# Gate matrices as two fp32r products per token in place of one fp32 product

## What is computed

```
cand = (v1[..., :, None] + v2[..., None, :]).reshape(T, PEER_HEADS, PEER_TOPK * PEER_TOPK)
sc, pos = lax.top_k(cand, PEER_TOPK)
e1 = jnp.take_along_axis(i1, pos // PEER_TOPK, axis=-1)
e2 = jnp.take_along_axis(i2, pos % PEER_TOPK, axis=-1)
experts = (e1 * PEER_NKEYS + e2).reshape(T, PEER_HEADS * PEER_TOPK)
gates = jax.nn.softmax(sc, axis=-1).reshape(T, PEER_HEADS * PEER_TOPK)
...
u = peer_u[ec]
a = jax.nn.gelu(jnp.einsum("ckd,cd->ck", u, hc).astype(jnp.float32)) * gc
vv = peer_v[ec]
return jnp.einsum("ck,ckd->cd", a.astype(vv.dtype), vv)
```

## Time and profile before

| | us |
|---|---|
| runs (3): median | 3059.06 |
| lowest, highest | 3058.15, 3063.45 |
| profiled execution, its own time | 3053.1 |
| its span | 3051.2 |
| first pass: gelu of tick 0 to gelu of tick 127 | 1821.87 to 2489.52 |
| TensorE, VectorE, ScalarE busy over the span | 2839.0, 2259.4, 1481.5 |

### The profile page before, as it was taken

The page is one execution under the profiler, slowest core; times in us unless marked ns, Lnnn a source line. Parts: engine busy times, 40 slices in busy tenths (PEclk is TensorE's granted clock), DMA queues, the critical chain, the costliest instruction groups (busy, mean ns, idle before and its releaser), DMA issues.

```text
span 3051.2 us, 37281 instructions
## 1 busy us (share of the span) xinstructions
PE 2839.0 (93%) x13623; PEld 2361.2 (77%) x13623; DVE 2259.4 (74%) x3019; ACT 1481.5 (49%) x1990; POOL 595.8 (20%) x478
## 2 busy tenths in 40 slices
PE   5979888999999879998999898999899989999998
PEld 3657756888888758776777678989899988888887
DVE  6465547888888753887854229999998868888886
ACT  4443236888788633544542433563756633333332
POOL 0200111111111100000000010033233444444442
PEclk7999998999999989999999999999999999999999
DMA  7544636999999633332333334477779999999995
GB/s 298 170 161 155 207 128 247 369 369 365 360 359 355 235 128 121 107 115 80 102 133 131 121 105 161 175 265 282 280 264 332 354 377 367 360 370 362 360 366 190
DMA packets 203692, 746.29 MB, mean 245 GB/s; under 512 B 24817, under 2 KB 78193, under 8 KB 146417
## 3 DMA queue, kind: packets, MB, share of 16 engines
q1 hardware_dynamic: 123568, 492.93, 44.8%
q0 software_dynamic: 56912, 179.26, 16.7%
q10 hardware_dynamic: 23024, 71.67, 6.1%
HBM read 670.80 MB, written 98.11 MB: 252 GB/s over the span
## 4 chain that ended last, share of the span: by engine, by line
PE 51%; DVE 19%; issue 6%; DMA 5%; ACT 4%; ACTq 0%; DVEq 0%; POOL 0%; POOLq 0%
PE PS L542 44%; DVE wlo L1856 4%; DMA gbuf<-in_peer_u_dram,IDX 3%; DVE hf L2606 2%; DVE oh L2592 2%; ACT whi L1194 1%; DVE hf L2618 1%; PE PS L996 1%; PE PS L1008 1%; PE PS L847 1%; ACT HH L1826 1%; PE PS L1121 1%; DVE zo L2362 1%; DVE sS L2645 1%; PE PS L1092 1%
## 5 line engine op out<-in xcount | busy, mean ns | idle before, releaser
L1856 DVE TENSOR_TENSOR wlo<-raw,whi 128x2048 fp32r<-128x2048 f32 x392 | 894.3, 2289 | 367.5 <-ACT whi L1194 330.8
L1194 ACT ACTIVATE whi<-raw 128x2048 fp32r<-128x2048 f32 x392 | 750.8, 1916 | 370.7 <-PE PS L542 310.3
L542 PE MATMUL PS<-HH,whi 128*128 128x512 f32 (+1 forms) x2056 | 790.0, 384 | 37.2 <-DVE wlo L1856 14.4
L542 PE MATMUL PS<-HH,wlo 128*128 128x512 f32 (+1 forms) x2056 | 754.2, 367 | 0.0
L542 PE MATMUL PS<-HL,whi 128*128 128x512 f32 (+1 forms) x2056 | 752.9, 366 | 0.0
L542 PEld LDWEIGHTS PS<-HH,whi 128*128 128x128 f32 x2056 | 392.4, 191 | 98.4 <-issue 21.2
L542 PEld LDWEIGHTS PS<-HL,whi 128*128 128x128 f32 x2056 | 392.4, 191 | 46.1 <-issue 7.7
L542 PEld LDWEIGHTS PS<-HH,wlo 128*128 128x128 f32 x2056 | 391.4, 190 | 42.9
L542 PE MATMUL PS<-whi,HH 128*128 128x512 f32 (+1 forms) x896 | 351.8, 393 | 22.0 <-DVE HL L2648 16.6
L542 PE MATMUL PS<-whi,HL 128*128 128x512 f32 (+1 forms) x896 | 347.1, 387 | 0.0
L542 PE MATMUL PS<-wlo,HH 128*128 128x512 f32 (+1 forms) x896 | 347.0, 387 | 0.0
(11 more groups left out here) (415 smaller groups left out, 3908.9 us busy)
## 6 DMA issues: line engine op xcount, KB each, us to landing
raw<-in_moe_dram SPq DMA_DIRECT2D x192, 1024.0 KB, 7.3
raw<-in_u_units_dram SPq DMA_DIRECT2D x64, 1024.0 KB, 6.5
raw<-in_v_units_dram SPq DMA_DIRECT2D x64, 1024.0 KB, 8.8
raw<-in_w_in_dram SPq DMA_DIRECT2D x44, 1024.0 KB, 5.2
raw<-in_w_ada_dram SPq DMA_DIRECT2D x24, 1024.0 KB, 5.7
acts_dram<-sS ACTq DMA_DIRECT2D x64, 384.0 KB, 5.7
gates_dram<-XT ACTq DMA_DIRECT2D x24, 1024.0 KB, 8.2
sS<-acts_dram SPq DMA_DIRECT2D x42, 384.0 KB, 7.3
```

The lines of the kernel that those rows point to most:

```text
L542: ins = t.matmul(dst, a, b, start=(first and n == 0), stop=(last and n == 2))
L1194: a.inc(a.e.activation(m.whi[p % HRING][:, :, :], m.raw[RAW_SLOT[load_of(p)]][:, :, :], ACT.Copy), "hi", p)
L1856: v.inc(v.e.tensor_tensor(m.wlo[h][:, :, :], m.raw[RAW_SLOT[load_of(p)]][:, :, :], m.whi[h][:, :, :].bitcast(F32), ALU.subtract), "lo_v", p)
```

## The change

- The weighting of a gate's first one-hot is made twice: with the weight's high half, written in place, and with its low half, written to the free columns of `HH` and `HL`. All one-hots are fp32r. TensorE multiplies both with the second one-hot and adds them up: two fp32r products in place of one fp32.
- For each tile, ScalarE makes an fp32r copy of the transposed weights, and VectorE subtracts it to get the low half (`glow`).
- The planner counts 700 instead of 1100 ns of TensorE for a gate step.
- A buffer (`e12`) shares the place of another; `eT` grows by 128 columns.

```diff
@@ peer_schedule
-            tensor += 1100
+            tensor += 700
@@ Plan
-                self.eT = [sb(s2, "eT", [128, 384]), self.rstd]
-                self.oh = sb(s2, "oh", [128, 4, 2, 4, 128])
+                self.eT = [sb(s2, "eT", [128, 512]), self.rstd]
+                self.oh = sb(s2, "oh", [128, 4, 2, 4, 128], F32R)
...
+    def oh_low(self, n, j):
+
+        return (self.HH, self.HL)[n % 4 // 2][:, 4 * (n % 2) + j, 0:TD]
@@ pe_gate_step
+            pe.wait_ge("glow", i - 1)
...
-            ins = t.matmul(m.PS[:, 5 + n % 3, 128 * k:128 * k + 128], m.oh[:, n % 4, 0, k, :],
-                           m.oh[:, n % 4, 1, k, :], start=True, stop=True)
+            for low, w in enumerate((m.oh[:, n % 4, 0, k, :], m.oh_low(n, k))):
+                ins = t.matmul(m.PS[:, 5 + n % 3, 128 * k:128 * k + 128], w, m.oh[:, n % 4, 1, k, :],
+                               start=(low == 0), stop=(low == 1))
@@ act_gate_step
+            a.wait_ge("weighted", 32 * (k - 1) - 1)
         a.inc(s.activation(m.eT[k % 2][:, 0:384], m.PS[:, 4, 0:384], ACT.Copy), "eT", i)
+        a.inc(s.activation(m.eT[k % 2][:, 384:512].bitcast(F32R), m.PS[:, 4, 256:384], ACT.Copy), "ghigh", i)
...
-        a.wait_ge("eT", TD // 128 + k)
+        a.wait_ge("glow", TD // 128 + k)
         for j in range(4):
             t = 256 + 4 * q + j
-            a.inc(s.activation(m.oh[:, n % 4, 0, j, :], m.oh[:, n % 4, 0, j, :], ACT.Copy,
-                               scale=m.eT[k % 2][:, t:t + 1]), "weighted_part" if j < 3 else "weighted", n)
+            row = m.oh[:, n % 4, 0, j, :]
+            a.inc(s.activation(m.oh_low(n, j), row.bitcast(F32), ACT.Copy, scale=m.eT[k % 2][:, t + 128:t + 129]),
+                  "weighted_part", n)
+            a.inc(s.activation(row, row.bitcast(F32), ACT.Copy, scale=m.eT[k % 2][:, t:t + 1]),
+                  "weighted_part" if j < 3 else "weighted", n)
@@ dve_gate_step
+        if q == 0:
+            v.wait_ge("ghigh", TD // 128 + k)
+            v.inc(v.e.tensor_tensor(eT[:, 384:512], m.PS[:, 4, 256:384], eT[:, 384:512], ALU.subtract), "glow",
+                  TD // 128 + k)
```

More of the change, by code:

```diff
@@ L223 @@
     "peer_a": "xrow sq5 root5",
-    "choice": "top pick gsub gt index onehot",
+    "choice": "glow top pick gsub gt index onehot",
     "conv_a": "mean csq cdev zaff zact fstep",
@@ L508, in __init__ @@
                 self.gt = sb(s2, "gt", [128, NT, 8, 16])
-                self.e12 = sb(s2, "e12", [128, 8, 16])
+                self.e12 = self.wkk[:, 0, :].rearrange("p (h k) -> p h k", h=8)
                 self.e1 = sb(s2, "e1", [128, NT, 8, 16])
@@ L2566, in dve_choice_step @@
         if i * 128 < TD:
-            v.inc(e.scalar_tensor_tensor(out=m.e12[:, :, :], in0=m.e1[:, i, :, :], scalar=128.0,
+            v.inc(e.scalar_tensor_tensor(out=m.e12, in0=m.e1[:, i, :, :], scalar=128.0,
                                          in1=m.e2[:, i, :, :], op0=ALU.mult, op1=ALU.add), "pick")
             v.own()
-            v.inc(e.tensor_copy(m.IDX[:, :].rearrange("p (h k) -> p h k", h=8), m.e12[:, :, :]), "index")
+            v.inc(e.tensor_copy(m.IDX[:, :].rearrange("p (h k) -> p h k", h=8), m.e12), "index")
         v.inc(e.tensor_tensor(G3, m.sc16[:, :, :], bass.AP(m.sc16, 0, [[128, 128], [16, 8], [0, 16]]),
@@ L2593, in dve_gate_step @@
                                 bass.AP(m.io128, 0, [[128, 128], [0, 2], [0, 4], [1, 128]]),
-                                bass.AP(eT, 4 * q, [[512 if k % 2 else 384, 128], [128, 2], [1, 4], [0, 128]]),
+                                bass.AP(eT, 4 * q, [[512, 128], [128, 2], [1, 4], [0, 128]]),
                                 ALU.is_equal), "onehot", n)
```

## The result

| | before | changed |
|---|---|---|
| runs | 4 | 4 |
| median, us | 3061.07 | 3098.20 |
| lowest, highest | 3058.15, 3063.45 | 3096.68, 3102.13 |
| ratio | | 1.0122, 95% interval 1.0107 to 1.0137 |

The change costs 37 us. The profiled execution took 3098.8 us, its span is 3096.9 us, 45.7 more than that of before. Of these, 8.6 us lie ahead of tick 0 (its gelu starts at 1830.44 instead of 1821.87), in stages that the change doesn't touch; the profiled execution of before was 6 to 8 us under its median, that of the change is on it. So the stretch is compared from the gelu of tick 0 on.

What follows compares the result with a forecast made beforehand. VectorE was taken to bound the pass to about tick 92, then TensorE; after the change ScalarE in two-step ticks. The pass's +26.7 us, with the turn +29.5, rounded to +30, gave 3089 us: forecast 3080 to 3100, range 3068 to 3116.

Steps and rivals of the forecast that it cites:

- What bounds: First expert pass, second block: VectorE sets the end to about tick 92, then TensorE; after the change ScalarE in two-step ticks.
- ScalarE over 95% busy: Sign that the forecast is right: ScalarE busy over 95% in ticks 68 to 83 and 105 to 122.
- TensorE's term: Gate products: 0.89 us a step instead of 0.85, 0.111 us a record, 3.8 us more over 96 steps.
- ScalarE's term: Second weighting, 0.293 us each: a pair of two-step ticks needs 15.1 us of ScalarE, up from 10.41.
- rival 2: VectorE's lumps and the new ScalarE chain add up, relief to tick 67 lost: 3119 us, chance 0.17.
- VectorE's relief: Ticks to 67: VectorE's choice work thinned out by the planner, tick 67 reached 24 us earlier.
- rival 1: ScalarE's second weighting is hidden, two-step ticks run at TensorE's 5.95 us, 54 us less: 3035 us, chance 0.06.
- The last ticks: End of the first pass: the last product and ticks 124 to 127 take 17.6 us.
- The planner's term: Price 700 for 1100: choice steps later, VectorE thinned out where it bound, 35 two-step ticks instead of 25.
- The turn: Turn to second pass: gates asked for later, landing in 14.2 us, taking the loss from +26.7 to +29.5 us.
- rivals 3 and 4: 3: thinning gives more, turn costs nothing, 3074 us, chance 0.15. 4: nothing measurable, 3059 us, chance 0.04.

Runs made afterwards that it cites:

- E8: Kernel before with the planner counting 1500 instead of 1100 for a gate step, exact products kept: 3074.04 us, ratio 1.0032.
- E10: Kernel before with the planner counting 1300 instead of 1100 for a gate step: 3078.63 us, ratio 1.0045.
- E7: Changed kernel with the planner counting 1500 instead of 700 for a gate step: 3074.14 us, ratio 1.0031.
- E3: Changed kernel without the low halves, neither their weighting on ScalarE nor their product on TensorE: 3068.09 us, ratio 1.0019.
- E2: Kernel before with the planner counting 700 instead of 1100, exact product and single weighting kept: 3073.68 us, ratio 1.0032.
- E6: Changed kernel with a third weighting, four more per gate step on ScalarE: 3182.5 us, ratio 1.0382.
- E5: Changed kernel with SyncE asking for the first stored activations ahead of the first gates at the turn of the passes: 3099.29 us, ratio 1.0113.
- E1: Changed kernel with the planner's price put back from 700 to 1100, halves kept: 3086.27 us, ratio 1.0079.
- E4: Changed kernel with 64 moving columns instead of 128 in the gate products: 3093.42 us, one execution.

## Why the prediction was right

The forecast was 3089 us, +30; measured were +37 and 3098 us, inside the 3080 to 3100 of the forecast, near their top.

- **What bounds**: right. VectorE up to the last choice step, then TensorE; after the change ScalarE in the two-step ticks. In E8 the same method, work shifted from VectorE's stretch and summed from rows, gave +21 in the pass and +21.1 was measured; E10, at +23 instead of +10, is where it didn't hold. Of the signs named, ScalarE over 95% busy did not come: 91 and 94%.
- **TensorE's term** (+3.8 us of work, 0.111 us a record): right. 0.11 us a record, and in the change's two-step ticks TensorE waited for ScalarE's copies. E7 and E8 tie although one has 0.89 us a step and the other 0.85; E3 with half the products gained some 4 to 6 us on E2.
- **ScalarE's term**: right to the digit for the pair (15.1 forecast, 15.00 measured; E6 19.7 and 19.66). The step that was a little short is the sum over ticks: 68 to 83 took 124.5 us, not 121, for the one wait of 3.5 us for a one-hot, a small piece of what rival 2 spoke of; 84 to 104 took 91.2 (90.6) and 105 to 122 133.1 (134); against that, VectorE's relief was 28 us at tick 67, not 24. What the second weighting costs in these 34 ticks was put too high beside rival 1, at 54 us: its bound of 5.95 us a tick is TensorE's work alone, and E2 shows 6.8 and 6.7, so it is 28 us (257.6 against 230.0). The sum had no use for that bound.
- **The last ticks**: from tick 122 to 127 21.4 us, not 17.6. Here I miscounted: five ticks of 4.17 were left, and the working had a product and four. The pass came out at +29.8 for +26.7, all of it this slip; that the rest came out even is luck, as the other terms were off by -4, +3.5, +0.6 and -1 us.
- **The planner's term**: the tick tables and the relief were right, but the prediction spoke of the new order as a relief with a price at ScalarE alone. E2 shows that it costs 10 us by itself: what is thinned out early returns late, as gathered rows and gate steps in an end whose DMA share is 0.95. This didn't spoil the sum, since the sum went tick by tick; it did spoil my expectation for E2, which took the relief as a gain that stays.
- **The turn**: mis-sized. +2.8 us forecast, +5.4 measured. The request went out 4.9 us after tick 125's gelu, as taken (5). It is the landing that was too short: 14.2 us, the median, were taken, and the gates took 16.6, inside the 12.2 to 17.8 of the earlier trace rows. The stored activations behind them on the same queue, left out of the sum, landed 1.0 us after them, and VectorE began 17.8 us after the gates' request. In E5, with the order turned round, it waited for the gates.
- Rival 1 (hidden weighting) came true only where VectorE is slower still (E7); rival 2's condition, the relief lost by tick 67, failed at 28 us; rivals 3 and 4, at 3074 and 3059, are well under what was measured.

So of the 37 us the halves make 24 (E1) and the order 10 (E2); the 3 left are within the intervals. Taken the other way round, the order adds 12 us to E1 and the halves 25 to E2.

## What to carry to other kernels

A product that gets cheaper isn't a gain until the engine that feeds it is counted: a split into halves moves work from TensorE to the engine that makes the halves, and 0.29 us for each small weighting outweighed whatever two reduced products might have saved over one exact one, which here was nothing. Price short instructions by the distance of their starts, for both engines, and add them up for the densest tick, not for the span: ScalarE, at 49% over the span before and 51% after, became the bound in 34 ticks of 128. A planner's cost is a lever on *where* work piles up, so look at the end of the stretch, at what is left over there and which transfers wait for its last mark; in this kernel the one edit that paid (8 rows moved over the turn) came from reading the wait at the turn, not from any product.

## What the runs showed of the hardware that was not expected

- An fp32r product with a weight of its own starts 0.11 us after the one before, at 64 moving columns as at 128 (E4), about the same as one of the two records of a plain fp32 product (0.106).
- ScalarE's weighting with a scale per partition, 128 columns: 0.39 us long, 0.293 from start to start, in four- and eightfold runs alike. The Trainium skill ("ScalarE: Activation LUTs", What ACT_TABLE_LOAD costs) gives 186 ns + 0.833 ns a column, about 93 more for a pointer operand, and an overlap of about 93: by this an estimate of 0.386 and 0.293 us. The trace agrees, with 0.39 and 0.293.
- TensorE's granted clock was lower in stretches in which it waited for ScalarE: 0.91 in ticks 69 to 83 after, 0.92 in ticks 63 to 76 of E1, against 0.98 in those of before. That is a share of the time at the lower level, 1.2 GHz. It cost nothing while ScalarE was last, as two pairs of ticks of the change behind one another show, the first at 1.00, the second at 0.89:

```profile
2433.97:2448.96 14.99, 12.30 (x82) 12.08 (x82) 12.05 (x14) 14.07 (x40) 5.90 (x5) 1.00 0.95 339
2448.96:2463.96 15.00, 12.28 (x72) 12.06 (x72) 12.10 (x15) 14.08 (x41) 6.32 (x5) 0.89 0.86 307
```
